# Time mixing with two 64-row by 128-column products per step in place of four 64x64 quarters

## The reference, cut to what matters

```python
xx = jnp.pad(h, ((0, 0), (1, 0), (0, 0)))[:, :-1] - h
xr, xw, xk, xv, xa, xg = [h + xx * mix[i] for i in range(6)]
r = (xr @ w_r).astype(f32)
k = (xk @ w_k).astype(f32)
v = (xv @ w_v).astype(f32)
...
_, y = lax.scan(rwkv7_step, jnp.zeros((B, H, N, N), f32), seqs)   # 16 heads of 64, 256 steps
...
return (y.astype(h.dtype) * g) @ w_o
```

## Time and profile before

| | |
|---|---|
| median of 3 runs | 2613.22 us |
| range of the runs | 2612.35 to 2615.81 us |
| the profiled execution's own time | 2614.25 us |
| span from its first to its last instruction | 2612.8 us |
| passes 0 to 2 of the time mixing, in that span | about 742 to 893 us |
| granted TensorE clock over the span | 0.998 |

### The profile page before, as it was taken

The page is one execution under the profiler, slowest core; times in us unless marked ns, Lnnn a source line. Parts: engine busy times, 40 slices in busy tenths (PEclk is TensorE's granted clock), DMA queues, the critical chain, the costliest instruction groups (busy, mean ns, idle before and its releaser), DMA issues.

```text
span 2612.8 us, 43958 instructions
## 1 busy us (share of the span) xinstructions
PE 2575.4 (99%) x17868; PEld 2222.7 (85%) x17868; DVE 2034.4 (78%) x2928; ACT 1605.1 (61%) x2362; POOL 238.3 (9%) x236
## 2 busy tenths in 40 slices
PE   8999999999999999999999999999999999999999
PEld 7999899999977779999888888888888888888887
DVE  6667676776766547678765788999999999999997
ACT  5557665555542235553555536887788778787875
POOL 1101000000111217001600100000000000000000
PEclk9999999999999999999999999999999999999999
DMA  7554355455322135563455545999999999999994
GB/s 271 182 188 146 114 183 178 174 208 180 140 99 68 51 131 192 180 220 107 161 189 193 181 151 205 373 373 347 362 364 364 354 352 371 365 365 361 373 365 156
DMA packets 85390, 609.69 MB, mean 233 GB/s; under 512 B 9608, under 2 KB 9864, under 8 KB 12224
## 3 DMA queue, kind: packets, MB, share of 16 engines
q1 hardware_dynamic: 82080, 594.58, 62.2%
q10 hardware_dynamic: 2752, 9.09, 0.9%
q0 software_dynamic: 352, 3.15, 0.3%
HBM read 605.73 MB, written 1.05 MB: 232 GB/s over the span
## 4 chain that ended last, share of the span: by engine, by line
PE 93%; DVE 4%; ACT 2%; issue 1%; DMA 0%; POOL 0%; ACTq 0%; DVEq 0%
PE bank L439 92%; PE bank L3305 1%; DVE weights_lo L429 0%; ACT weights_hi L421 0%; ACT squares L478 0%; DMA x_T<-in_x 0%; DVE mean L580 0%; POOL squares L975 0%; PE bank L2178 0%; DVE rstd L496 0%; DVE weights_hi_scratch L2295 0%; DVE weights_hi_scratch L2362 0%; DVE weights_lo_scratch L2295 0%; DVE arena L589 0%; DVE x_T L905 0%
## 5 line engine op out<-in xcount | busy, mean ns | idle before, releaser
L429 DVE TENSOR_TENSOR weights_lo<-raw_weights,weights_hi 128x1024 fp32r<-128x1024 f32 x816 | 1002.8, 1249 | 357.6 <-ACT weights_hi L421 352.3
L421 ACT CAST weights_hi<-raw_weights 128x1024 fp32r<-128x1024 f32 x816 | 847.6, 1050 | 300.6 <-PE bank L439 281.0
L439 PE MATMUL bank<-source,weights_hi 128*128 128x512 f32 (+1 forms) x2464 | 613.5, 365 | 13.6 <-ACT weights_hi L421 10.0
L439 PEld LDWEIGHTS bank<-source,weights_hi 128*128 128x128 f32 x2464 | 412.7, 190 | 60.2 <-ACT weights_hi L421 10.0
L439 PE MATMUL bank<-weights_hi,source 128*128 128x512 f32 (+1 forms) x1280 | 387.1, 386 | 1.5 <-DVE source L663 1.0
L439 PE MATMUL bank<-source,weights_lo 128*128 128x256 f32 x2112 | 380.5, 282 | 0.0
L439 PEld LDWEIGHTS bank<-source,weights_lo 128*128 128x128 f32 x2112 | 338.3, 190 | 37.8 <-DVE weights_lo L429 0.6
L429 DVE TENSOR_TENSOR weights_lo<-arena,weights_hi 128x1024 fp32r<-128x1024 f32 x278 | 335.9, 1223 | 30.6 <-ACT weights_hi L421 27.1
L421 ACT CAST weights_hi<-arena 128x1024 fp32r<-128x1024 f32 x278 | 292.2, 1053 | 50.6 <-PE bank L439 36.0
L439 PEld LDWEIGHTS bank<-weights_hi,source 128*128 128x128 f32 x1280 | 231.6, 188 | 44.9 <-issue 3.1
L439 PE MATMUL bank<-weights_lo,source 128*128 128x512 f32 (+1 forms) x640 | 243.4, 380 | 0.0
(11 more groups left out here) (352 smaller groups left out, 3396.2 us busy)
## 6 DMA issues: line engine op xcount, KB each, us to landing
raw_weights<-in_exp_in SPq DMA_DIRECT2D x134, 1024.0 KB, 5.4
arena<-in_exp_in SPq DMA_DIRECT2D x90, 1024.0 KB, 5.6
raw_weights<-in_exp_w SPq DMA_DIRECT2D x67, 1024.0 KB, 5.8
arena<-in_exp_w SPq DMA_DIRECT2D x45, 1024.0 KB, 5.4
raw_weights<-in_ffn_w_down SPq DMA_DIRECT2D x44, 1024.0 KB, 4.8
raw_weights<-in_ffn_w_up SPq DMA_DIRECT2D x43, 1024.0 KB, 4.8
raw_weights<-in_ffn_w_gate SPq DMA_DIRECT2D x42, 1024.0 KB, 4.8
raw_weights<-in_dense_w SPq DMA_DIRECT2D x33, 1024.0 KB, 4.8
```

Of the source, the lines that this page charges most:

```text
L421: k.act.copy(k.weights(j)[0], raw_half(k, j)).then_inc(k.w_hi_ready, 1)
L429: k.dve.tensor_tensor(lo, raw_half(k, j), hi.bitcast(F32), ALU.subtract).then_inc(k.w_ready, 1)
L439: return k.pe.matmul(dst, lhsT, rhs, start=start, stop=stop, skip_group_check=shared)
```

## The change

In passes 0 to 2 each projection step is made as two products of 64 rows and 128 output columns, one for each row half, where there were four of 64 rows and 64 columns. Banks, their sums, the order of steps, the waits and the weight loads stay as they are. The number of fp32 products per step falls from four to two.

```diff
-def project_quadrants_tensor(k, t, use, name, u, which):
+def project_halves_tensor(k, t, use, name, u, which):
 
     w = k.raw_unit(name, u)
     k.pe.wait_ge(*k.landed(k.unit[name, u]))
     banks = [claim_bank(k, (use, u)), claim_bank(k, (use + "2", u))]
     for j in range(2):
         for kt in range(KT):
-            for h, c in QUADRANTS:
-                at = kt * CHUNK + j * P + c * HEAD
-                ins = mm(k, banks[h][part(c), j * T:(j + 1) * T], w[part(h), at:at + HEAD], blk(t.xm[which], kt)[part(h), :],
-                         kt == 0, kt == KT - 1, True)
+            for h in range(2):
+                ins = mm(k, banks[h][:, j * T:(j + 1) * T], w[part(h), kt * CHUNK + j * P:kt * CHUNK + (j + 1) * P],
+                         blk(t.xm[which], kt)[part(h), :], kt == 0, kt == KT - 1, True)
             if j == 1 and kt == KT - 1:
                 ins.then_inc(*k.raw_taken.step((name, u)))
             yield
```

More of the change, by code:

```diff
@@ L1674, in dense_tensor @@
     if u < UNITS:
-        keys = project_quadrants_tensor(k, t, "K", "rw_wk", u, MIX_K)
+        keys = project_halves_tensor(k, t, "K", "rw_wk", u, MIX_K)
         yield from steps(keys, 8)
@@ L1682, in dense_tensor @@
         yield from keys
-        rate = project_quadrants_tensor(k, t, "R", "rw_wr", u, MIX_R)
+        rate = project_halves_tensor(k, t, "R", "rw_wr", u, MIX_R)
         yield from steps(rate, KT)
@@ L1689, in dense_tensor @@
         yield
-        yield from project_quadrants_tensor(k, t, "V", "rw_wv", u, MIX_V)
+        yield from project_halves_tensor(k, t, "V", "rw_wv", u, MIX_V)
     else:
```

## The result

The change makes the kernel slower: 2630.76 us (median of 4 runs, 2630.15 to 2631.49) against 2612.78 (2610.94 to 2615.81), a ratio of 1.0065 with a 95% interval of 1.0053 to 1.0077. That is 18.0 us more; 21.9 were forecast. The profiled execution took 2631.49 us, its span is 2630.0.

A forecast was written before the change was run, and what follows sets the result against it. TensorE (PE), busy 99% of the span, was taken to bound the kernel. Blocks add 23.4 us, waits take back 0.37 and 1.14, leaving 21.9: 2636.2 for the profiled execution, 2635 against the median, range 2622 to 2642.

The forecast's parts named there:

- term 0: Projection steps of passes 0 to 2: two halves take 0.43 us like four quarters, so halving the products gains nothing.
- Rival 3: Halves accumulating into two banks do not run side by side: 62 us more, 2697 us; chance 0.02.
- A border between 64*64 and 64*128: Change of tile shape between pair products and projection halves: taken as 0.20 us each, bounds 0 and 0.20 plus 0.05.
- Rival 1: No border between 64*64 and 64*128 tiles, so not slower: 2612 to 2616 us; chance 0.08.
- The blocks, 7.81 us a pass: Added length of a pass's 24 projection blocks, new against old: 7.81 us, 23.4 us over three passes.
- What waits take back, 1.51 us: Waits for DVE swallow 0.37 us in round 0 of pass 0 and 0.57 in round 4 of passes 1 and 2.
- Stalls put down to issue: Fewer records could shorten stalls of 0.70 and 1.15 us: bounds 0 and 1.9 us of gain, taken as 0.
- Rival 2: Waits for the pair chain on DVE and ACT end most rounds and swallow half: +11 us, 2624; chance 0.10.
- Rival 4: Borders cost more, 0.25 us a change over 39 new changes a pass: 6 us more, 2641; chance 0.10.

The follow-up runs named there:

- e5: The kernel before the change, unchanged, profiled once more: 2614.75 us, one run.
- e6: The kernel after the change, unchanged, profiled once more: 2629.64 us, one run.
- e9: The kernel after the change, unchanged, timed on another chip: 2632.5 us, ratio 1.0076 to the kernel before.
- e1: From the kernel after, each projection step is one product of 128 rows and 128 columns: 2624.47 us against 2614.05 for the kernel before.
- e2: From the kernel after, only V is projected in halves, K and R in quarters: 2618.9 us against 2614.05 for the kernel before.
- e8: From the kernel after, only each block's first projection step is in halves, the others in quarters: 2635.91 us against 2612.98 for the kernel before.

## Why the prediction was right

Direction, mechanism and range were right; the time was 4.2 us too high (2635 against 2630.8). Point by point:

- *Pace, term 0.* Right. Eight 64*128 records inside a block take 1.13 us, (1.13 - 0.376 - 0.10) / 3 = 0.218 us a pair. Rival 3 (halves one behind the other, 2697) did not come.
- *A border between 64*64 and 64*128.* No row before showed this pair. It costs what the others do: 0.15 us in, 0.31 out, and 0.10 and 0.05 of open load, the same within 0.001 us in all 54 entries from small pair products. The rule of the Trainium skill (TensorEngine Tiling (Array Packing), Tiling Modes, Key Properties), that a change of tiling mode drains TensorE, agrees with these rows. Rival 1 (2612 to 2616) is out. The count of 39 changes a pass was exact (117 counted).
- *The blocks, 7.81 us a pass.* Mis-sized. Round 12 came out at 0.52, rounds 15 and 19 at 0.40, round 6 at 0.20, as forecast to the hundredth. But rounds 3 and 5, forecast at 0.32, measured 0.13 and 0.16, and rounds 2, 18 and 24 came out 0.05 lower. The step that failed is that I measured the old block from the last pair product on, as if the pairs' own part stayed as it was. It became shorter: in round 3 from 1.05 us (first to last start, 754.27 to 755.32) to 0.91. In the old order it overlapped the projections at both ends. At its start the last quarters of the block before still ran, and at its end two projection quarters had slipped in ahead of the last pair products; the start held the pairs up by 0.08 us and the end by 0.06. In the kernel before:

```profile
753.58 1.06 PE L439 MATMUL bank<-arena,raw_weights 64*64 64x256 f32 x14
754.27 0.37 PE L439 MATMUL bank<-weights_hi_scratch,squares 64*64 64x32 f32 x8
```

  The sum without stalls is about 7.25, 0.56 less a pass, 1.7 in all.
- *What waits take back, 1.51 us.* Right in kind, short in size. DVE's work over rounds 0 to 3 of pass 1 runs from 800.46 to 811.01 in the kernel after, 10.55 us against 10.56 from 794.68 to 805.24:

```profile
800.46 1.29 DVE L2294 TENSOR_TENSOR weights_hi_scratch<-bank,arena 128x512 f32<-128x512 f32 x2 [4.29 <-PE bank L439]
...
811.01 0.24 DVE L2318 TENSOR_TENSOR weights_hi_scratch<-weights_hi_scratch,bank 128x128 f32<-128x128 f32 x1
```

  PE's product of round 4 starts without a wait at 812.36, 0.31 after the last half, in place of the wait in the earlier trace rows:

```profile
811.30 1.13 PE L439 MATMUL bank<-arena,raw_weights 64*128 64x256 f32 x8
812.36 0.66 PE L439 MATMUL bank<-weights_hi_scratch 64*64 64x32 f32 x16
```

  The 0.57 us were taken in both passes, and 0.25 more in round 1, where a wait that I had not read took in the lateness: 0.5 us in all.
- *Stalls put down to issue, bounded at 0 to 1.9 us of gain and taken as 0*. In the two profiled executions they gave 1.9 us. 21.9 - 1.7 - 0.5 - 1.9 = 17.8, which is what the stage took. e5 and e6 show that this term belongs to the execution in part; zero was not the best value between the ends, but no row could have told.
- *Rival 2* (most rounds end in waits, +11) is out: the loads' waits for DVE fell by 4.0 us over the three passes, and most rounds took their whole added time.
- *Rival 4* (0.25 a border, 2641) is out: a block of two steps is 1.21 us from start to start and 0.05 of open load, 1.26 as summed.

## What to carry to other kernels

Where small tiles of different work alternate in short blocks, keep one tile shape through all of it, even if that takes twice the instructions: here four quarters and two halves ran at the same pace, and a border cost 0.12 to 0.18 us of the kernel's time. Count changes of shape in program order before ranking groups by busy time; the group that caused this loss got cheaper by that measure. The way round paid too, if by little: a block-diagonal full-tile product between quarter products was better made as its quarters (e7, 2.1 us, interval 0.3 to 5).

## What the runs showed of the hardware that was not expected

TensorE's granted clock fell for a few microseconds in some executions of the same kernels. Windows of PE in e9 (length, busy, granted clock, DMA share, GB/s):

```profile
748.20:749.70 1.50, 1.50 (x17) 0.57 0.00 0
749.70:752.70 3.00, 3.00 (x18) 0.65 0.02 5
752.70:755.70 3.00, 3.00 (x48) 1.00 0.00 0
```

In the profile of before the same stretch has 1.00 throughout. It is the lower of the two levels, 1.2 GHz in place of 2.4: pairs of halves started 0.41 to 0.43 us apart and not 0.216. PE had just had three waits for DVE in round 0 and 1 (starts 1.36, 0.49 and 0.49 us apart). From 749.7 to 752.7 e1, e2 and e5 show it too (0.50, 0.59 and 0.65), and in e5 the stretch was 1.5 us longer than in before; before, after and e6, with the same waits, do not have it. It is worth 1.5 us in one execution, about as much as e7 gains, so a change of that size can't be judged from one profile.

The same happens once more just behind the stage. At the start of pass 3 PE of the kernel before was busy for only 1.96 of 4.20 us, and then its granted clock was at the lower level for 3.4 us:

```profile
892.80:897.00 4.20, 1.96 (x68) 1.00 0.71 240
897.00:900.40 3.40, 3.11 (x9) 0.50 0.04 17
```

After has this too (915.0 to 918.4), so it is no part of the 18.0 us. But e1, e6, e8 and e9 do not have it, and there everything behind the stage took 1717.7 to 1718.9 us, against 1719.2 to 1720.1 in the other profiles.

That a stall without a releaser keeps its place and length in one spot (1.37 us at 820) and comes and goes in others was not expected either; what ends it was not tried. Nor was a kernel run in which the transpositions too are made in quarters.
